# Two transformer blocks on one core of Trainium2: the constants split around x, a sum in the RWKV preparation moved, attention bias added by VectorE, loads and tables reordered

## What is computed

```
# RWKV-7, per head of 64 (32 heads)
kk = k * k_k;  kk = kk / max(norm(kk), 1e-12)          # sum of squares, root
k  = k * (1 + (a - 1) * k_a)
... scan over time gives y, group norm of y ...
bonus = sum(r * k * r_k, over the head) * v            # a second sum over the head
y = (y + bonus) * g
# mixing of the two branches of block one
h = sigmoid(gates[:D]) * branch_a + sigmoid(gates[D:]) * branch_b
x = alpha * x + rmsnorm(h @ w_out)                      # rmsnorm: a root over the mean square
# NSA attention, 16 heads of 64: window scores with a relative-position bias
s = q @ k.T * scale + bias[head, query - key]           # then softmax, gate, @ v
# the end: layernorm of alpha * x + ffn(x)
```

## Time and profile before

| | |
|---|---|
| median of 3 runs | 4057.66 us (4056.7 to 4057.76) |
| profiled execution: time / span | 4059.71 / 4057.9 us |
| PE busy | 3884.5 us, 96% |
| PE weight loads | 3570.9 us, 88% |
| DVE / ACT / POOL busy | 1750.4 / 597.1 / 1244.5 us |
| bytes moved | 665.70 MB, mean 164 GB/s |

### The profile page before, as it was taken

How to read it: one execution, slowest core, us unless ns; L and a number is a source line. 1 busy time by engine, 2 the same in 40 slices (tenths; PEclk the granted TensorE clock), 3 DMA queues, 4 the chain that set the end, 5 groups by cost and what they waited for, 6 DMA issues and landing times.

```text
span 4057.9 us, 65356 instructions
## 1 busy us (share of the span) xinstructions
PE 3884.5 (96%) x28308; PEld 3570.9 (88%) x28308; DVE 1750.4 (43%) x3171; ACT 597.1 (15%) x1310; POOL 1244.5 (31%) x795
## 2 busy tenths in 40 slices
PE   8999999999999898999999999999998899999997
PEld 7788888888878898999999998777697899999997
DVE  1343426551122523111125446642422588878544
ACT  0233311111111011000000010222302211111001
POOL 0000000003221765777750000000251477775000
PEclk9999999999999999999999999999999999999998
DMA  6556554447564443444444454434342344444541
GB/s 229 191 195 219 210 219 156 178 162 236 176 193 173 155 148 107 171 173 172 168 162 160 163 205 166 153 129 130 64 159 87 123 167 167 167 167 162 172 160 69
DMA packets 106927, 665.70 MB, mean 164 GB/s; under 512 B 22992, under 2 KB 27424, under 8 KB 76176
## 3 DMA queue, kind: packets, MB, share of 16 engines
q1 hardware_dynamic: 61904, 544.81, 37.4%
q0 software_dynamic: 21200, 70.80, 5.9%
q10 hardware_dynamic: 23536, 45.92, 3.1%
HBM read 611.34 MB, written 50.13 MB: 163 GB/s over the span
## 4 chain that ended last, share of the span: by engine, by line
PE 92%; DVE 3%; ACT 2%; issue 1%; DVEq 1%; POOL 0%; ACTq 0%; DMA 0%; POOLq 0%
PE product_bank L548 48%; PE product_bank L596 30%; PE product_bank L390 3%; PE mixer_bank L734 1%; PE mixer_bank L750 1%; PE mixer_bank L2176 1%; ACT xT L851 0%; PE mixer_bank L2177 0%; PE mixer_bank L1263 0%; DVE arena L1349 0%; PE mixer_bank L1277 0%; PE mixer_bank L1114 0%; PE mixer_bank L2208 0%; PE mixer_bank L1096 0%; PE mixer_bank L2141 0%
## 5 line engine op out<-in xcount | busy, mean ns | idle before, releaser
L596 PE MATMUL product_bank<-hT,weight_ring 128*128 128x256 f32 x3648 | 817.4, 382 | 0.0
L596 PEld LDWEIGHTS product_bank<-hT,weight_ring 128*128 128x128 f32 x3648 | 693.7, 191 | 105.1 <-issue 10.2
L548 PE MATMUL product_bank<-hT,weight_ring 128*128 128x128 f32 x3680 | 457.0, 276 | 12.8 <-DVEq L1613 5.8
L548 PEld LDWEIGHTS product_bank<-hT,weight_ring 128*128 128x128 f32 x3680 | 435.5, 193 | 15.0 <-DVEq L1613 6.0
L548 PE MATMUL product_bank<-arena,weight_ring 128*128 128x128 f32 x3200 | 398.5, 275 | 0.0
L548 PEld LDWEIGHTS product_bank<-arena,weight_ring 128*128 128x128 f32 x3200 | 378.5, 192 | 0.6
L572 DVE TENSOR_TENSOR arena<-product_bank,arena 128x128 f32<-128x128 f32 x127 | 36.9, 291 | 739.4 <-PE product_bank L548 739.4
L2576 DVE SCALAR_TENSOR_TENSOR arena<-arena 128x256 f32<-128x256 f32 x176 | 321.7, 1866 | 14.7 <-ACT arena L2541 11.4
L515 POOL TENSOR_TENSOR arena<-weight_ring 128x1024 f32<-128x1024 f32 x89 | 209.7, 2356 | 361.6 <-PE product_bank L548 298.2
L518 POOL TENSOR_TENSOR weight_ring<-weight_ring 128x1024 f32<-128x1024 f32 x111 | 272.8, 2458 | 0.0
L548 PE MATMUL product_bank<-hT,arena 128*128 128x128 f32 x2048 | 250.3, 276 | 0.9 <-DVE hT L504 0.9
(11 more groups left out here) (496 smaller groups left out, 5362.2 us busy)
## 6 DMA issues: line engine op xcount, KB each, us to landing
weight_ring<-in_weights SPq DMA_DIRECT2D x213, 2048.0 KB, 8.1
weight_ring<-in_weights SPq DMA_DIRECT2D x128, 512.0 KB, 5.7
weight_ring<-in_weights SPq DMA_DIRECT2D x64, 384.0 KB, 5.7
units<-out_stage ACTq DMA_DIRECT2D x87, 256.0 KB, 7.9
rwkv_keep<-arena ACTq DMA_DIRECT2D x16, 1282.0 KB, 7.1
arena<-units POOLq DMA_DIRECT2D x52, 256.0 KB, 4.2
arena<-rwkv_keep POOLq DMA_DIRECT2D x8, 1280.0 KB, 7.6
arena<-units POOLq DMA_DIRECT2D x48, 128.0 KB, 6.0
```

The lines of the kernel that those rows point to most:

```text
L548: mm = pe.matmul(bank[:, at * P:at * P + P], lhs[:, j, :], rhs[:, j, :], start=g == 0 and n in (0, 3) and j == 0, stop=g == n_groups - 1 a ...
L596: mm = pe.matmul(psg[b][:, half * T:half * T + T], lhs, rhs, start=k == 0, stop=k == 15)
```

## The change

The diff is cut to its core; the numbering of lines shifts by 2 to 30 in the changed kernel.

```diff
 load_inputs (POOL)
+            first = CONST_AT["ones_mean"][1]
-            pool.dma_start(consts[:, :], t_in["consts"]).then_inc(sem("consts_loaded"), 16)
+            pool.dma_start(consts[:, 0:first], t_in["consts"][:, 0:first]).then_inc(sem("x_loaded"), 16)
             pool.dma_start(params[:, :], t_in["params"]).then_inc(sem("params_loaded"), 16)
+            pool.dma_start(consts[:, first:], t_in["consts"][:, first:]).then_inc(sem("consts_loaded"), 16)
 SP's program
-            sp.wait_ge(sem("x_loaded"), 16)
-            sp.wait_ge(sem("consts_loaded"), 16)
+            sp.wait_ge(sem("x_loaded"), 32)
+            sp.wait_ge(sem("params_loaded"), 16)
 ACT, new; called at the start and ahead of out_act, ffn_out_act, out2_act, ln_act 2, down_act
+        def root_table_act(act):
+            act.activation(small[:, 8:9], small[:, 0:1], ACT.Sqrt)
 rw1, PE
                 pe.matmul(pm[0][:, 0:256], const("head_ones"), rw["sq"], start=True, stop=True)\
                     .then_inc(sem("rw1_kk_sum"), 1)
+                yield
                 pe.wait_ge(sem("rw1_norm"), b1)
                 pe.wait_ge(sem("rw1_cum"), b1)
                 pe.matmul(pm[0][:, 256:512], const("head_ones"), rw["rk"], start=True, stop=True)\
                     .then_inc(sem("rw1_bonus_sum"), 1)
-                yield
                 pe.wait_ge(sem("rw1_operands"), b1)
 stream_weights (SP)
+                if n == UNIT_AT["branch_b0", 0][0] + RING - 1:
+                    gate_loads(sp)
 gates (was POOL, now SP), and the constants behind the fifth sum
-        def gates_pool(pool):
-            stage_stored(pool, "gates")
+        def gate_loads(sp):
+            stage_stored(sp, "gates")
+            sp.wait_ge(sem("rw2_group_done"), RW_TILES // GT)
...
+                if n == 4:
+                    nsa_consts_pool(pool)
 NSA, POOL
-            pool.dma_start(bias_rows, n_rows[0:16, 0:384]).then_inc(sem("bias_rows_stored"), 16)
+            pool.dma_start(bias_rows.rearrange("h (p n) -> h p n", p=P), n_rows[0:16, 0:384].unsqueeze(1).to_broadcast([16, P, 384]))\
+                .then_inc(sem("bias_rows_stored"), 16)
...
                 if h >= 2:
-                    pool.wait_ge(sem("attn_scores"), NSA_AT_HEAD + h - 1)
+                    pool.wait_ge(sem("nsa_biased"), 2 * (h - 1))
+                if h in (4, 10):
+                    pool.wait_ge(sem("compress_steps"), 2)
+                    sum_weights(pool, "out2", h // 10, 0, o2_sums_of(h // 10))
 NSA, PE
-                    pe.matmul(bank[w][:, 0:384], nc_("flip"), nbias[:, h % 2, :], start=True, stop=False)
-                    pe.matmul(bank[w][:, 0:256], q[:, P:T], k, start=False, stop=False)
-                    pe.matmul(bank[w][:, 256:384], q[:, 0:P], k[:, 0:P], start=False, stop=True)
+                    pe.matmul(bank[w][:, 0:256], q[:, P:T], k, start=True, stop=True)
+                    pe.matmul(bank[w][:, 256:384], q[:, 0:P], k[:, 0:P], start=True, stop=True)
 NSA, DVE (the bias is divided by HSCALE once; maxima are read from n_s instead of PSUM)
+                dve.wait_ge(sem(f"nsa_bias{h % 2}"), 32 * (h // 2 + 1))
                 for w in range(2):
+                    dve.tensor_tensor(n_s[:, 384 * w:384 * w + 384], bank[w][:, 0:384], nbias[:, h % 2, :], ALU.add)\
+                        .then_inc(sem("nsa_biased"), 1)
 NSA, ACT (the exponentials are two calls; the copy of the output stands between them)
                 if h + 1 < NH:
-                    exponentials(h + 1)
+                    exponentials(h + 1, 0)
                 act.wait_ge(sem("attn_out"), NSA_AT_HEAD + h + 1)
                 act.activation(hT[r, 8 + b, :], bank[0][r, 0:256], ACT.Copy).then_inc(sem("attn_head_done"), 1)
+                if h + 1 < NH:
+                    exponentials(h + 1, 1)
 out2, POOL
-            for u in range(8):
-                if u >= 2:
-                    group_used(pool, "out2", u - 2, 0)
+            for u in range(2, 8):
+                group_used(pool, "out2", u - 2, 0)
 the end, POOL
-            pool.wait_ge(sem("ln_done"), 3 * NCK)
-            pool.dma_start(t_out, xT[:, :, :]).then_inc(sem("out_written"), 16)
+            for c, ck in enumerate(chunks_of):
+                pool.wait_ge(sem("ln_done"), 2 * NCK + c + 1)
+                pool.dma_start(t_out[:, ck, :], xT[:, ck, :]).then_inc(sem("out_written"), 16)
```

More of the change, by code:

```diff
@@ L720, in squares_act @@
             for c, ck in enumerate(chunks_of):
-                act.wait_ge(sem(ready), count - NCK + 1 + c if ready != "x_loaded" else 16)
+                act.wait_ge(sem(ready), count - NCK + 1 + c if ready != "x_loaded" else 32)
                 act.activation(sq[:, ck, :], src[:, ck, :], ACT.Square).then_inc(sem("norm_squares"), 1)
+        def root_table_act(act):
+            act.activation(small[:, 8:9], small[:, 0:1], ACT.Sqrt)
         def root_act(act, tag, bank, eps_col):
@@ L2243, in nsa_act, with exponentials @@
             act.activation(ng, ng, ACT.Sigmoid).then_inc(sem("nsa_gates"), 1)
-            def exponentials(h):
+            def exponentials(h, w):
                 n_s, n_pt, n_cs, n_ct, n_st = nsa_bufs[h % 2]
                 act.wait_ge(sem("attn_max"), NSA_SOFT_AT + h + 1)
-                for w in range(2):
-                    for qb, (a, z) in enumerate([(256, 384), (0, 256)]):
-                        n = 2 * w + qb
-                        s = n_s[:, 384 * w + a:384 * w + z]
-                        act.activation(s, nsa_banks(h)[w][:, a:z], ACT.Exp, scale=HSCALE, bias=n_st[:, 8 + n:9 + n],
-                                       accum_out=n_st[:, 16 + n:17 + n])
+                for qb, (a, z) in enumerate([(256, 384), (0, 256)]):
+                    n = 2 * w + qb
+                    s = n_s[:, 384 * w + a:384 * w + z]
+                    act.activation(s, s, ACT.Exp, scale=HSCALE, bias=n_st[:, 8 + n:9 + n],
+                                   accum_out=n_st[:, 16 + n:17 + n])
+                if w == 0:
+                    return
                 for qb in range(2):
@@ L2257, in exponentials @@
                 act.drain().then_inc(sem("attn_exp"), 1)
-            exponentials(0)
+            exponentials(0, 0)
+            exponentials(0, 1)
             for h in range(NH):
@@ L2303, in nsa_dve @@
                 dve.tensor_tensor(cs, cs, cadd, ALU.add)
+                dve.wait_ge(sem(f"nsa_bias{h % 2}"), 32 * (h // 2 + 1))
                 for w in range(2):
-                    dve.reduce_max(n_st[:, 2 * w:2 * w + 1], bank[w][:, 256:384], AX.X)
-                    dve.reduce_max(n_st[:, 2 * w + 1:2 * w + 2], bank[w][:, 0:256], AX.X)
+                    dve.tensor_tensor(n_s[:, 384 * w:384 * w + 384], bank[w][:, 0:384], nbias[:, h % 2, :], ALU.add)\
+                        .then_inc(sem("nsa_biased"), 1)
+                dve.drain()
+                for w in range(2):
+                    dve.reduce_max(n_st[:, 2 * w:2 * w + 1], n_s[:, 384 * w + 256:384 * w + 384], AX.X)
+                    dve.reduce_max(n_st[:, 2 * w + 1:2 * w + 2], n_s[:, 384 * w:384 * w + 256], AX.X)
                 dve.drain()
@@ L2695, in _ @@
             gates_act(act)
+            root_table_act(act)
             out_act(act)
```

26 lines of the change are left out of this document (14 added, 12 removed).

## The result

The changed kernel takes 4035.58 us (median of 5 runs, 4030.8 to 4042.77) against 4057.76 us before: 0.9946 of the time, 95% interval 0.9932 to 0.9961. So it is faster, by 22 us, where 41 were forecast, and 1.6 us outside the range of 4001 to 4034. The runs spread over 12 us; those of the kernel before over 3. The profiled execution is the fastest of the five (4030.8 us, span 4028.9), 29.0 us shorter in span than that of before.

A forecast was written before the change was run, and what follows sets the result against it. PE was taken as the bound, holding 92% of the chain that ended last. Gains 24 + 1.6 + 1.1 + 11 + 3.2 + 0 = 41 off 4059.7 gave 4018.8, or 4016 us for the median; range 4001 to 4034.

The forecast's parts named there:

- Rival 2: NSA heads get slower, weight sums block DVE and PE's gaps halve the clock: 12 us over forecast, 4029; chance 0.2.
- Rival 3: Branch b: constants behind the fifth sum bring back the full standstill, 8 us above the charge, 4025; chance 0.1.
- A: RWKV sum: 22.4 us of waits and 6.8 of slow clock removed, 4.8 charged for new stalls; gain 24 us.
- B: Kernel start: fewer constants ahead let PE start at 11.05 us; gain 1.6 us, bounds 0 and 3.05.
- C: Root table loads move ahead of the sum; only the one behind `out` of block one counts; gain 1.1 us.
- D: Branch b start: without DMAs ahead POOL's first weight sum is hidden; 15.1 us gross, 4 charged, net 11.
- E: End of the kernel: output stored in pieces while ACT still works; gain 3.2 us, bounds 2 and 4.5.
- F: NSA heads: bias moves from PE to DVE, the bound moves from PE at 9.64 to a chain at about 9.3; gain 5.
- G: Weight sums of `out2` beside the heads: 6.5 us each, 13 in all, 5 us more than before.
- The lock: Beside G: VectorE and GpSimd share a port pair exclusively; the new additions, with one PSUM input, would not be locked out.
- H: Bias store of 3.1 MB before the heads: 10 us to 80 us, up to some 45 us free; taken as hidden.

The follow-up runs named there:

- e7: The kernel before with the move of the RWKV sum alone; 4027.55 us, 0.9929 of before.
- e6: The kernel of e1 with one more POOL drain, ahead of the wait that holds the first weight sum of branch b; 4009.8 us.
- e1: The changed kernel with ACT again making all exponentials of the next head ahead of its copy of this head's output; 4013.87 us, 0.9897 of before.
- e3: The changed kernel with the bias added by PE as before and exponentials again ahead of the copy, out2 sums still beside the heads; 4029.74 us.
- e5: The kernel of e1 with the first two weight sums of out2 also behind all heads; 4011.92 us, 0.9889 of before.
- e4: The kernel of e3 with the first two weight sums of out2 also back behind the heads; 4017.24 us.
- e2: The changed kernel with the first two weight sums of out2 back behind all heads' bias loads; 4035.58 us.
- e9: The kernel of e1 with the two out2 weight sums split into eight single operations, one in each of eight heads, behind a drain; 4008.83 us.
- e10: The kernel of e9 with the early drain of e6 and branch b's constants loaded behind the last weight sum; 3998.06 us, 0.9858 of before.

## Why the prediction was wrong

The direction was right; the time was 1.6 us outside the range, and the gain about half of the forecast. Rival 2 (heads slower by 12 us, PE's gaps halving its clock) is what happened. Rival 3 did not: behind the constants the standstill cost less than was charged. But one remained at the first weight sum, which no rival named.

- **A, the RWKV sum: 24 forecast, 28.6 in the trace, 29.3 alone (e7).** The mechanism was right, with the slow clock behind the long waits. The 4.8 us charged for new stalls were too much: the transposes stretch by 0.1 to 0.3 us in a tile, and of the 22.4 + 6.8 = 29.2 us of waits and clock all but 0.6 came back.
- **B, the start: 1.6 forecast, 1.5 at PE's first matmul, 2.6 behind `lora`.** Right.
- **C, the tables: 1.1 forecast, nothing kept.** The root behind `out` of block one (`mix_post`) comes right behind PE's mean, and the lead grows from 37.4 to 38.5 us at the next sums of squares. But these 32 matmuls then take 9.95 us instead of 9.13, at a granted clock of 0.72 instead of 0.78, and the lead is 37.5 again at the product behind them. The table's part of the forecast was right; that PE's clock would take it back was not in the sum. At the last layernorm the lead rises by 1.2 us, where I had put nothing: the same 32 sums take 8.86 us instead of 10.09, so it is the clock and not the table.
- **D, branch b: 11 forecast, 6.2 in the trace** (lead 31.2 to 37.4). The step that failed here is "without DMAs ahead the four operations start near 1310 and end near 1320". I put the 13.04 us standstill down to the DMAs in flight, and with the 22 issues gone I counted none. But 6.70 us of it stayed although the last issue was 90 us old, and PE waited 4.45 us; they went only when an earlier drain took them (e6). The 4 us charged for the sixth sum were somewhat high: 2.5 us of wait, and 2.7 of lead.
- **E, the end: 3.2 forecast, 3.4 in the trace** (lead 25.6 at the last root, 29.0 at the end). 2.9 us to landing in place of 6.6. Right.
- **F, the heads: this is the step that failed.** I had "the copy ends at 5.2; the other half and the compressed ones 1.4: 6.6; norm and scaling 2.6: 9.2 us". The 5.2 was read in heads in which PE never waited. It held in every second head (5.4, and 9.4 us from start to start). Once DVE is the bound PE waits 0.7 to 2.2 us in every undisturbed head, behind each wait of 2.2 us its clock falls, its output comes up to 1.8 us later, and through ACT's order this lateness goes back into the chain that PE waits for: the copy ends at 7.0, and the head takes 10.8 to 11.3 us. So a pair took 20.3 to 20.7 us where 18.6 were forecast, and a loss came where 5 us of gain stood. e1, which changes ACT's order and nothing else, takes off 22 us, as its expectation said to within 1 us; 21.4 of them lie in the heads of the two traces. That is more than the lateness, since the order itself also cost: without it a pair takes 16.9 us. The additions on DVE themselves, without that tie, are a gain: e1 against e3, with the sums beside the heads, is 15.9 us less, and e5 against e4, with the sums behind them, 5.3 (the intervals of these two, 0.9876 to 0.9903 and 0.9888 to 0.9918, overlap; 7.0 us lie in the heads of their traces).
- **G, the sums: 5 us of loss forecast.** From the distances, the two sums cost 6.4 and 4.3 us over undisturbed pairs, where the one at the end cost 6.6 before: a loss of 4. But against e2 moving them costs nothing, since at the end they would now cost 12. The size was right; the comparison with before mixed F and G. The lock that the prediction names beside G is borne out for operations with two SBUF inputs (e9); no new addition of the changed kernel falls under a POOL operation, so for them it wasn't tested.
- **H, the store: hidden, as forecast.** 36.7 us, between the 10 and the 80 of the bounds. By the Trainium skill's 104 GB/s ("SBUF — State Buffer", Door 1: The DMA port swizzle) it would be an estimated 30 us; the trace shows 3.1 MB in 36.7 us, 86 GB/s, beside the loads of SP's queue.
- The median lies 4.8 us above the profiled run, before 2.1 below it. The spread of 12 us shrinks to 4 in e1; that the falls of the clock in the heads make it is likely but was not shown, since only one run of the changed kernel, the shortest, has a trace.

The surplus of A (4.6 us) happens to cover the shortfall of D (4.8): that the kernel stood on the forecast up to the heads is in part luck.

What stays open: what POOL's drain waits for behind DMA issues, and why PE's clock differs between traces of the same code (3.5 us between e1 and e9 from 2400 to 2740 us), which limits what a single trace can tell.

## What to carry to other kernels

A wait for another engine in the middle of a work item that a third engine needs whole makes a ring of all three: put the whole of the piece that someone waits for first, and the copy that frees a buffer behind it. When work moves from the bound engine to a chain that was just below it, the new period can't be read from the old one, because times of the old bound engine were measured while it never waited, at full clock. Split helper work into single operations and place each in the idle time of the engine with which it collides, and pay for a drain where its engine is idle anyway.

## What the runs showed of the hardware

- At the first drain of GpSimd behind DMA issues of its own queue, GpSimd stood 13.04 us behind 22 fresh issues, 6.70 us when the last of them was 90 us old, 4.1 to 4.8 us behind six fresh ones, 2.9 and 1.1 us in the heads of the changed kernel, and 1.7 to 4.6 us in those of e9 and e10. An earlier drain took the 6.70 us away completely (e6).
- A wait of TensorE of 2.33 us after fully busy stretches halved the granted clock in four of eight cases that look alike, and cost 1.7 us each time on top of the wait. In the undisturbed heads of the changed kernel the clock was at half behind each of the five waits of 2.17 to 2.18 us, and at full behind those of 0.65 to 1.02 us.
- GpSimd operations of 2.34 us held up VectorE operations of 0.17 to 0.19 us with two SBUF inputs, and a tensor-scalar one, until their own end, to 1.94 to 2.27 us, but not a reduction and a reciprocal.
